# Hybrid attention layer on one core: where the logits of the next unit stand among the transposes of the turned probabilities

## The reference

```
logits = einsum('bqhd,bkhd->bhqk', qb, k) * scale      # 128 queries x up to 1024 keys
logits = logits + bias ; masked to the causal keys
p = softmax(logits)                                    # exp and division by the sum
out = einsum('bhqk,bkhd->bqhd', p, v)
```

## Time and profile before

| | |
|---|---|
| median of 3 runs | 1423.17 us (1423.05 to 1423.25) |
| the profiled execution, its own time | 1423.14 us |
| its span, first to last instruction | 1420.8 us |
| PE busy | 1396.7 us, 98% of the span |
| PE weight loads (PEld) busy | 1116.9 us, 79% |
| DVE busy, ACT busy | 722.7 us (51%), 697.0 us (49%) |
| mixer A's attention | about 642 to 880 us of the span |
| mixer B's attention | about 880 to 1144 us of the span |

### The profile page before, as it was taken

The page is one execution under the profiler, slowest core; times in us unless marked ns, Lnnn a source line. Parts: engine busy times, 40 slices in busy tenths (PEclk is TensorE's granted clock), DMA queues, the critical chain, the costliest instruction groups (busy, mean ns, idle before and its releaser), DMA issues.

```text
span 1420.8 us, 21098 instructions
## 1 busy us (share of the span) xinstructions
PE 1396.7 (98%) x7910; PEld 1116.9 (79%) x7910; DVE 722.7 (51%) x1647; ACT 697.0 (49%) x1539; POOL 67.5 (5%) x132
## 2 busy tenths in 40 slices
PE   7999999999999999999999999999999999999998
PEld 6987777777777888887777777777777788888886
DVE  6557745455667785564333444633433345222734
ACT  7467866666753451115555565555454522112323
POOL 3133000000000000000000000000000000000000
PEclk9999999999999999999999999999999999999999
DMA  6154111111111122221101021112222131232522
GB/s 215 30 142 112 30 37 31 38 30 38 30 38 38 49 63 82 74 79 48 31 23 31 23 68 53 38 38 60 68 84 80 53 104 45 60 96 62 175 89 104
DMA packets 107059, 92.07 MB, mean 65 GB/s; under 512 B 8528, under 2 KB 93904, under 8 KB 106704
## 3 DMA queue, kind: packets, MB, share of 16 engines
q1 hardware_dynamic: 97824, 58.22, 15.3%
q0 software_dynamic: 9136, 32.52, 7.2%
HBM read 70.53 MB, written 15.99 MB: 61 GB/s over the span
## 4 chain that ended last, share of the span: by engine, by line
PE 94%; DVE 2%; ACT 1%; issue 1%; PEld 1%; POOL 1%; DMA 0%; PEldq 0%; POOLq 0%; DVEq 0%; ACTq 0%
PE bank L905 22%; PE bank L907 22%; PE bank L906 22%; PE bank L1084 7%; PE bank L1103 6%; PE slot L1074 4%; PE slot L1059 2%; PE slot L905 2%; PE slot L906 2%; PE slot L907 2%; PE slot L1018 1%; PE bank L1028 1%; DVE slot L1704 0%; PE bank L923 0%; PE bank L1142 0%
## 5 line engine op out<-in xcount | busy, mean ns | idle before, releaser
L905 PE MATMUL bank<-hs,w_hl 128*128 128x512 f32 x1088 | 434.8, 400 | 1.2 <-DVE tm L1798 0.8
L907 PE MATMUL bank<-hs,w_hl 128*128 128x512 f32 x1088 | 424.8, 390 | 0.0
L906 PE MATMUL bank<-hs,w_hl 128*128 128x512 f32 x1088 | 423.8, 390 | 0.0
L1495 DVE TENSOR_TENSOR w_hl<-w_raw,w_hl 128x512 fp32r<-128x512 f32 (+1 forms) x168 | 113.8, 679 | 267.9 <-ACT w_hl L1194 266.7
L907 PEld LDWEIGHTS bank<-hs,w_hl 128*128 128x128 f32 x1088 | 204.2, 188 | 44.4
L905 PEld LDWEIGHTS bank<-hs,w_hl 128*128 128x128 f32 x1088 | 204.5, 188 | 41.9 <-issue 2.7
L906 PEld LDWEIGHTS bank<-hs,w_hl 128*128 128x128 f32 x1088 | 204.8, 188 | 38.7
L1194 ACT ACTIVATE w_hl<-w_raw 128x512 fp32r<-128x512 f32 (+1 forms) x168 | 103.9, 620 | 156.7 <-PE bank L907 149.0
L1522 DVE TENSOR_SCALAR_CACHE_REDUCE idle_out<-score,state 128x768 uint8<-128x768 f32 (+3 forms) x140 | 115.3, 824 | 4.8
L1704 DVE CUSTOM_DVE_ANT_0 slot<-slot,score 128x128 f32<-128x128 f32 (+7 forms) x64 | 47.4, 781 | 67.4 <-PE slot L1074 67.1
L1397 ACT ACTIVATE idle_out<-score,state 128x896 bf16<-128x896 f32 x64 | 70.2, 1098 | 11.7 <-DVE state L1518 10.3
(11 more groups left out here) (322 smaller groups left out, 2205.7 us busy)
## 6 DMA issues: line engine op xcount, KB each, us to landing
w_raw<-in_w_in_dram SPq DMA_DIRECT2D x136, 256.0 KB, 2.8
merged_scratch<-ms POOLq DMA_DIRECT2D x16, 512.0 KB, 3.5
ms<-merged_scratch POOLq DMA_DIRECT2D x16, 512.0 KB, 4.0
xn<-in_x_dram SPq DMA_DIRECT2D x8, 512.0 KB, 5.8
iq_st<-iq_hl POOLq DMA_DIRECT2D x32, 128.0 KB, 2.8
w_raw<-in_w_o_dram SPq DMA_DIRECT2D x16, 256.0 KB, 3.3
qb_scratch<-bq_raw POOLq DMA_DIRECT2D x4, 512.0 KB, 2.9
w_raw<-in_w_c_dram SPq DMA_DIRECT2D x8, 256.0 KB, 2.7
```

Source lines behind the costliest of these rows:

```text
L905: pe.matmul(out_, wh, mh, start=start, stop=False)
L906: pe.matmul(out_, wh, ml, start=False, stop=False)
L907: return pe.matmul(out_, wl, mh, start=False, stop=stop)
L1495: v.tensor_tensor(lo, src, hi.bitcast(F32), ALU.subtract).then_inc(w_low, 1)
```

## The change

The order of `between` places is changed in `pair_run`: the logits of unit s stand right behind the pv of unit s-2, and all groups of unit s-1 follow in one piece.

```diff
@@ -232,16 +232,13 @@
             if s >= 2:
                 units[s - 2]["pv"] = ring()
                 plan.append(("pv", units[s - 2]))
+            if between:
+                logits()
             if 1 <= s <= n:
                 x = units[s - 1]
                 parts = [(hh, c) for hh in range(2) for c in range(x["W"] // P)]
                 x["groups"] = [dict(parts=parts[g0:g0 + 4]) for g0 in range(0, len(parts), 4)]
-                if between:
-                    turn(x, slice(0, 2))
-                    logits()
-                    turn(x, slice(2, None))
-                else:
-                    turn(x, slice(0, None))
+                turn(x, slice(0, None))
             if s < n:
                 plan.append(("exp", units[s]))
                 if units[s]["br"] == "c" and s % 2 == 1:
```

## The result

The changed kernel takes 1430.95 us (median of 4 runs, 1430.85 to 1431.0), the kernel before 1423.16 (4 runs, 1423.05 to 1423.25): a ratio of 1.0055, 95% interval 1.0037 to 1.0072, so 7.8 us **slower**. The span of the profiled execution rose from 1420.8 to 1428.5 us, by 7.7.

What follows compares the result with a forecast made beforehand. PE's issue was taken to bound the kernel (busy 98% of the span); +15.0 - 5.1 - 2.4 = +7.5 us on 1423.14 gave 1430.6 us. The 8-in-10 range was 1425.5 to 1436 us.

Steps and rivals of the forecast that it cites:

- Term 1: PE at 30 places: one pv-to-logits gap (0.17 us, bounds 0.07 and 0.37) replaces two of 0.17; saves 5.1 us.
- Term 2: PE's waits for ACT's late copies before or within the first eight transposes, at eight places, get covered; saves 2.4 us.
- Term 3: Third transpose group waits for ACT's copy of the first: 0.48 us a place, 0.52 with four groups; costs 15.0 us.
- The exponentials: Softmax on ACT beside the transposes: second exponential ends 3.2 us behind the last transpose, 0.6 us more slack, no new wait.
- That the wait is not paid: Rival: ACT's copies keep up, third group idles under 0.25 us a place; faster, 1415.6 us; chance 0.06.
- That it evens out: Rival: pv-to-logits gap of 0.07 and shorter third-group wait; within 2.8 us of before, about 1424.6; chance 0.09.
- That the exponentials come late: Rival: exponentials queue behind four ACT copies, next logits wait 0.3 us at 22 places; 6.6 us on top, 1437; chance 0.04.
- A fall of the clock: Rival: PE runs at 1.2 instead of 2.4 GHz in longer transpose runs; 42 us more, 1472; chance 0.01.
- a load done ahead: Third group's weights loaded during its wait: 0.14 us a place, 4 us in all back, sum about +3; rows spoke against it.

Runs made afterwards that it cites:

- The control: The run with three matmuls, but with those three moved to between the logits and the first group: 1432.89 us, ratio 1.0068 to the kernel before.
- the run with one group: Kernel before, with one group of transposes instead of two ahead of the logits: 1427.03 us, ratio 1.0027.
- the run with three matmuls: Changed kernel, with the next projection piece's first three matmuls put between second and third group at 29 places: 1416.95 us, ratio 0.9956 to the kernel before.

## Why the prediction was right

The prediction said 1430.6 us, slower; the median is 1430.95.

- **What bounds the kernel.** PE's issue, gap by gap. The sum of gaps on PEld explains the whole change of the span (below), while DVE's and ACT's busy times moved by at most 3 us with no effect.
- **Term 1, one change of kind less (5.1 us).** The open price was the gap from pv to logits. It measures 0.17 us at all 30 places, the value taken, not the 0.07 or 0.37 of its bounds. The reason given for it is only half of one. Width alone does not set the gap: the logits of the earlier trace rows are 128 columns wide too and leave 0.07. What pv shares with the transposes beside the width is that the kernel gives both plain float32 operands, and the logits float32r. No run separates the two, so the value was a choice between two rows that came out well.
- **Term 2, waits covered by the logits (2.4 us).** All eight are gone. Terms 1 and 2 show in the fall of the "issue" waits from 24.3 to 18.2 us, 5.1 of it term 1 and 0.9 term 2, and in the missing waits of 0.70 and 0.84 us.
- **Term 3, the third group's wait (15.0 us).** It measures 15.6 - 1.0 = 14.6 us at the 30 places (0.48 to 0.49 each), and the fourth group adds 0.05 us at 14 places (0.69 us for six transposes where the earlier trace rows has 0.64), 0.7 us: 15.3 in all. The control, the run with one group and the run with three matmuls show the cause: the round of one bank through ACT, 1.35 us from the first transpose, against 0.87 us of transposes.
- **The sum.** 15.3 - 5.1 - 2.4 = 7.8 us, against 7.7 in the span and 7.8 between the medians. The forecast was 7.5.
- **The exponentials.** Expected: no new wait, 0.6 us more slack behind the last transpose. After the change the second exponential at block 7's logits ends at 701.62, 3.06 us behind the last transpose (698.56), against 3.84 before and 3.2 forecast: 0.8 us sooner. PE first needs it for the transposes at 703.66, since the short logits at 703.18 take one slot and wait for the first exponential only. That is a slack of 2.04 us, where it was 702.43 - 701.66 = 0.77. The timelines of ACT and of PEld:

```profile
697.22 1.08 ACT L1376 ACTIVATE pta<-bank 128x512 f32<-128x512 f32 x2 [1.90 <-PE bank L1081]
698.56 0.87 ACT L1376 ACTIVATE pta<-bank 128x512 f32<-128x512 f32 x2 [0.26 <-PE bank L1081]
699.32 1.12 ACT L1366 ACTIVATE pa<-slot,nmax 128x1024 f32<-128x1024 f32 x1
...
701.40 0.22 ACT L1366 ACTIVATION_READ_ACCUMULATOR pa<-slot,nmax 128x1 f32 x1
...
703.18 0.41 PEld L1071 LDWEIGHTS slot<-ka,qa 64*128 64x128 f32 x6 [0.17 <-issue]
703.66 0.85 PEld L1081 LDWEIGHTS bank<-ident,pa 128*128 128x128 f32 x8
```

  The exponential follows the copies without a gap, where in the earlier trace rows it had waited for DVE: the earlier logits did help DVE, and ACT had become the limit of that chain, as worked out.
- **The rivals.** That the wait is not paid falls with the 0.48 to 0.49 us of every place; its point of decision was 0.25. That it evens out falls with the same wait and with the gap of 0.17. That the exponentials come late falls with the slack above. A fall of the clock does not show: the granted clock is 1.00 in both mixers' windows:

```profile
642.00:883.00 241.00, 235.71 (x1719) 184.84 (x1718) 96.75 (x235) 134.43 (x308) 3.78 (x7) 1.00 0.13 35
883.00:1152.00 269.00, 264.09 (x1833) 207.51 (x1832) 109.80 (x220) 131.97 (x305) 10.03 (x19) 1.00 0.21 61
```

  The Trainium skill says ("TensorE: Matmul & The Clock Gate", Part 4) that transposes don't count as busy the way matmuls do. These rows show no effect of it, with up to 16 transposes in a run. The other rule of the Trainium skill that was weighed, that PE's queue pulls weight loads ahead of matmuls ("TensorE: Matmul & The Clock Gate", Part 2), did not shorten the wait either: PEld stays idle for all of it, and the term came out at 15.3 us rather than the 11 that a load done ahead would have left.

For the gaps that the change does save, the Trainium skill states a cause: by "TensorEngine Tiling (Array Packing)", Key Properties, a change of tiling mode drains the engine. The rows agree with it. pv is 128x64, logits 64x128, transposes and projections 128x128, and apart from waits the gaps stand just where these change: 0.17 us behind pv and behind transposes, none between transposes and projections. No run here changes the shape alone, so this cause is not shown.

## What to carry to other kernels

With two banks in turn, count what stands between a bank's filling and its next use on the filling engine: it has to last as long as the bank's round through the engine that empties it (here 1.35 us from the first transpose), or the difference is paid each time. Work that looks misplaced in the middle of a run may be that filler; when it is moved out, something else must move in, best something of the same shape of weights (here 128x128, between which the rows show no gap), and only as much as the wait is long. And when a trace contains the new order somewhere already, even twice at the ends of the loops, read its price there.

## What the runs showed of the hardware

Transposes that follow projections show no gap, but their first ones are slower: eight take 1.03 us behind projections (control run) against 0.86 behind logits, and four take 0.58 instead of 0.42 in the run with three matmuls between. This row is from the latter, a place with three groups:

```profile
686.88 0.58 PEld L1099 LDWEIGHTS bank<-ident,pa 128*128 128x128 f32 x4
```

About 0.1 us of it is given back where the projections' first loads follow transposes closer than the usual 0.227 us (696.33 to 696.44 above). What is left, 1.9 us over 29 places in the control, is 0.07 us for each excursion to projections and back, where I had allowed 0.04 at most. In the run with three matmuls between, the same allowance was rather too large, since its sum came out 0.4 us over the measured time.
